# Residual rows of the first LayerNorm added to the expert sums inside rounds 0 and 1, and the routing lists made in one go

## The reference, cut to what matters

```python
x  = layer_norm(ALPHA * x + g1 * mix, ln1_g, ln1_b)          # x1, the residual rows spoken of below
u2 = x * (1 + sc2) + sh2
x  = layer_norm(ALPHA * x + g2 * hier_moe(u2, ...), ln2_g, ln2_b)

def hier_moe(u, ...):          # top-1 group of 4, then top-2 of its 8 experts; 32 experts in all
    g_idx = argmax(softmax(h @ w_gr + b_gr)); e_logits = h @ w_er + b_er
    top_val, top_idx = top_k(e_logits[group g_idx], 2)
    gate = g_w * softmax(top_val)
    for e in range(N_EXPERTS):
        hid = silu(h @ w_gate[e]) * (h @ w_up[e])            # 2048 -> 512
        y = y + dense_gate[:, e:e+1] * (hid @ w_down[e])     # 512 -> 2048
```

## Time and profile before

| | |
|---|---|
| time of the profiled execution, its span | 1728.13 us, 1726.0 us |
| median of three runs | 1728.73 us |
| TensorE matmul busy, share of span | 1568.4 us, 91% |
| VectorE busy | 532.8 us, 31% |
| ScalarE busy | 203.7 us, 12% |
| GpSimd busy | 88.4 us, 5% |
| moved by DMA, mean rate over the span | 537.01 MB, 311 GB/s |
| mean granted TensorE clock | 0.963 of 2.4 GHz |
| chain that ended last | PE 71%, DMA 17%, DVE 5% |

### The profile page before, as it was taken

How to read it: one execution, slowest core, us unless ns; L and a number is a source line. 1 busy time by engine, 2 the same in 40 slices (tenths; PEclk the granted TensorE clock), 3 DMA queues, 4 the chain that set the end, 5 groups by cost and what they waited for, 6 DMA issues and landing times.

```text
span 1726.0 us, 24825 instructions
## 1 busy us (share of the span) xinstructions
PE 1568.4 (91%) x9617; PEld 896.4 (52%) x9617; DVE 532.8 (31%) x948; ACT 203.7 (12%) x343; POOL 88.4 (5%) x174
## 2 busy tenths in 40 slices
PE   3799999999999998999977999999989889899893
PEld 0256666535777754577745444444435444344351
DVE  0110029611322324422164332323223232232325
ACT  0000010200000013320043000000000000100002
POOL 3000000000111100010001000000000000000000
PEclk8799999999999899899987999999999999999997
DMA  9999988875444363454336999999999999999991
GB/s 362 422 416 400 370 316 318 324 292 209 158 135 153 132 221 121 172 207 153 137 152 243 361 419 409 415 425 424 414 400 418 399 417 415 406 424 419 418 386 61
DMA packets 79394, 537.01 MB, mean 311 GB/s; under 512 B 10385, under 2 KB 10561, under 8 KB 18065
## 3 DMA queue, kind: packets, MB, share of 16 engines
q1 hardware_dynamic: 72146, 507.62, 73.5%
q0 software_dynamic: 6576, 26.35, 4.5%
q10 hardware_dynamic: 624, 2.36, 0.3%
HBM read 533.40 MB, written 11.80 MB: 316 GB/s over the span
## 4 chain that ended last, share of the span: by engine, by line
PE 71%; DMA 17%; DVE 5%; SPq 3%; ACT 2%; issue 2%; ACTq 0%; DVEq 0%
PE ps L616 15%; PE ps L1165 14%; DMA ring<-w_gate 12%; PE ps L1008 7%; PE ps L1190 6%; PE ps L629 6%; PE ps L600 4%; PE ps L1147 3%; SPq L407 3%; DMA ring<-w_ada 3%; DMA arena<-w_in 2%; PE ps L686 2%; PE ps L662 1%; PE ps L1117 1%; DVE arena L2037 1%
## 5 line engine op out<-in xcount | busy, mean ns | idle before, releaser
L1165 PE MATMUL ps<-ring,arena 128*64 128x256 f32 x3200 | 358.8, 383 | 21.2 <-DMA ring<-w_gate 20.0
L1165 PEld LDWEIGHTS ps<-ring,arena 128*64 128x64 f32 x3200 | 227.6, 138 | 167.8 <-DMA ring<-w_gate 33.3
L616 PE MATMUL ps<-arena,ring 128*128 128x288 f32 x1024 | 256.9, 409 | 0.0
L616 PEld LDWEIGHTS ps<-arena,ring 128*128 128x128 f32 x1024 | 191.9, 190 | 69.7 <-issue 18.4
L1190 PE MATMUL ps<-arena 128*64 128x512 f32 x800 | 181.5, 601 | 20.2 <-DVE arena L2055 12.9
L600 PE MATMUL ps<-ring,silu_c 128*32 128x512 f32 x768 | 103.7, 658 | 38.0 <-POOLq L513 19.4
L1008 PE MATMUL ps<-arena,ring 128*128 128x288 f32 x512 | 124.7, 406 | 0.0
L1190 PEld LDWEIGHTS ps<-arena 128*64 128x64 f32 x800 | 54.5, 138 | 131.2 <-issue 93.0
L629 PE MATMUL ps<-ring,arena 128*128 128x512 f32 x256 | 117.0, 605 | 1.3 <-ACT arena L1263 0.7
L1147 PE MATMUL ps<-arena 64*128 64x512 f32 x384 | 104.5, 636 | 12.3 <-DVE arena L2037 10.7
L1008 PEld LDWEIGHTS ps<-arena,ring 128*128 128x128 f32 x512 | 97.2, 190 | 26.8
(11 more groups left out here) (451 smaller groups left out, 1263.0 us busy)
## 6 DMA issues: line engine op xcount, KB each, us to landing
ring<-w_gate SPq DMA_DIRECT2D x100, 1024.0 KB, 23.5
ring<-w_up SPq DMA_DIRECT2D x100, 1024.0 KB, 25.8
arena<-w_down SPq DMA_DIRECT2D x100, 1024.0 KB, 26.4
ring<-w_ada SPq DMA_DIRECT2D x96, 1024.0 KB, 10.6
ring<-w_in SPq DMA_DIRECT2D x52, 1024.0 KB, 6.5
ring<-w_o SPq DMA_DIRECT2D x16, 1024.0 KB, 6.3
ring<-cache_k SPq DMA_DIRECT2D x16, 512.0 KB, 4.4
ring<-cache_v SPq DMA_DIRECT2D x16, 512.0 KB, 4.3
```

The source lines that it names most:

```text
L616: last = mm(ps[:, bank, 0:T], ring[:, slot, P * t:P * (t + 1)], uT[:, t, :], start=(t == 0), stop=(t == KC - 1))
L1165: last = mm(ps[B * s:B * (s + 1), 2 + c // 4, 0:256], xgT[:, 4 * (c % 4) + t, :], ring[:, c, 512 * t + 256 * s:512 * t + 256 * (s + 1)], s ...
```

## The change

1. VectorE makes the sample columns of each quarter of u2 right behind that quarter (`gain_sample(0)` first), not one quarter later.
2. TensorE makes the count product ahead of token turns 10 and 11, not behind turn 11.
3. The 12 turns of x1 leave the routing. The list product follows the token turns at once.
4. The expert of each block is counted on 41 partitions, one per block, and turned to a row by a small TensorE product with the identity; `plan` is written from that, now behind `idxs`.
5. GpSimd clears `acc[0]` and `acc[1]` (two more memsets behind that of `xg`). The turns of x1 stand at the end of round 0 (eight: rows 0 to 127 and the sample rows) and of round 1 (four: rows 128 to 255), in banks 4 and 7; VectorE adds them, times ALPHA, into `acc` or writes the sample rows, and TensorE waits for the last of them before it goes on to the next round.
6. `ln2b` is fetched by SyncE's queue behind the last expert, not by GpSimd's before the rounds. Buffers move in SBUF accordingly.

```diff
@@ buffers (some of them) @@
-        xgT = area(6656, KC, B)
+        xgT = area(18432, KC, B)
...
-        ln2b = area(18432, 2, D)
+        ln2b = area(4608, 2, D)
...
-        eid = rta(1624, NB1, parts=1)
-        ecmp = area(13824, NB1, NE, parts=1)
+        eid = rta(1624, 1)
+        ecmp = rta(1625, NE)
@@ SyncE, behind the loop over the experts @@
+            sp.wait_ge(tt_pe, 24)
+            sp.dma_start(ln2b, ln2.partition_broadcast(P)).then_inc(ln2_loaded, 16)
@@ GpSimd @@
             link(g.memset(xg, 0.0))
+            g.memset(acc[0], 0.0)
+            g.memset(acc[1], 0.0).then_inc(acc_clear, 1)
             pool.wait_ge(plan_ready, 1)
...
             gather(1)
-            pool.wait_ge(tt_pe, 24)
-            pool.dma_start(ln2b, ln2.partition_broadcast(P)).then_inc(late_loaded, 16)
@@ TensorE, routing @@
             for n in range(1, 12):
+                if n == 10:
+                    pe.wait_ge(rt_dve, 1)
...
                 turn_tokens(n, u2T)
...
-            for n in range(12, 24):
-                if n < 16:
-                    pe.wait_ge(x1_act, 4 * (n - 12) + 4)
-                if n == 16:
-                    pe.wait_ge(rt_dve, 2)
...
-                turn_tokens(n, rT)
+            pe.wait_ge(rt_dve, 2)
...
+            pe.wait_ge(rt_dve, 3)
+            mm(ps[0:1, 5, 0:NB1], eid[0:NB1, :], ident[0:NB1, 0:NB1], start=True, stop=True).then_inc(rt_pe, 1)
@@ TensorE, rounds @@
+            def turn_x1(first, i):
+                t0, tn = TILES[i]
+                for q in range(4):
+                    x = first + q
+                    if x >= 2:
+                        pe.wait_ge(xr_dve, x - 1)
+                    for m in range(4):
+                        last = nc.tensor.transpose(ps[0:tn, (4, 7)[x % 2], P * m:P * (m + 1)],
+                                                   rT[:, 4 * q + m, t0:t0 + tn], ident[:])
+                    last.then_inc(tt_pe, 1)
...
                         last.then_inc(moe_used, 1)
+                    with pe.If(i < 1):
+                        pe.wait_ge(x1_act, KC)
+                        turn_x1(0, 0)
+                        turn_x1(4, 2)
+                        pe.wait_ge(xr_dve, 8)
+                    with pe.If(i > 0):
+                        with pe.If(i < 2):
+                            turn_x1(8, 1)
+                            pe.wait_ge(xr_dve, 12)
@@ ScalarE @@
-            for n in range(12, 20):
...
-                A(xres[0:tn, i, :].rearrange("t (p m) -> t m p", m=KC)[:, 4 * q:4 * q + 4, :],
-                  ps[0:tn, 6 + n % 2, :].rearrange("t (m p) -> t m p", m=4), ACT.Copy, scale=ALPHA
-                  ).then_inc(tt_act, 1)
@@ VectorE @@
+            gain_sample(0)
             for q in range(1, 4):
                 centre(q)
                 scale_rows(q)
-                gain_sample(q - 1)
-            gain_sample(3)
+                gain_sample(q)
...
-            link(v.tensor_tensor(ecmp, bc(cum[0:1, :], 1, NB1), bc(iotab[0:1, 0:NB1], 2, NE), ALU.is_le))
+            link(v.tensor_scalar(ecmp, cum, tokid[:, 0:1], None, ALU.is_le))
             link(v.tensor_reduce(eid, ecmp, AX, ALU.add))
-            link(v.tensor_scalar(eid, eid, NE - 1.0, None, ALU.min))
-            v.tensor_copy(plan[0:1, 0:NB1], eid)
-            v.tensor_copy(plan[0:1, NB1:NB1 + 1], cum[0:1, NE - 1:NE]).then_inc(plan_ready, 1)
+            v.tensor_scalar(eid, eid, NE - 1.0, None, ALU.min).then_inc(rt_dve, 1)
             dve.wait_ge(rt_pe, 4)
...
+            dve.wait_ge(rt_pe, 5)
+            v.tensor_copy(plan[0:1, 0:NB1], ps[0:1, 5, 0:NB1])
+            v.tensor_copy(plan[0:1, NB1:NB1 + 1], cum[0:1, NE - 1:NE]).then_inc(plan_ready, 1)
...
+            def x1_rows(first, i):
+                for q in range(4):
+                    x = first + q
+                    dve.wait_ge(tt_pe, 13 + x)
+                    src = ps[0:TILES[i][1], (4, 7)[x % 2], :].rearrange("t (m p) -> t m p", m=4)
+                    if i == 2:
+                        v.tensor_scalar(xsrow.rearrange("t (p m) -> t m p", m=KC)[:, 4 * q:4 * q + 4, :], src,
+                                        ALPHA, None, ALU.mult).then_inc(xr_dve, 1)
+                    else:
+                        w = acc[i].rearrange("t (p m) -> t m p", m=KC)[:, 4 * q:4 * q + 4, :]
+                        v.scalar_tensor_tensor(w, src, ALPHA, w, ALU.mult, ALU.add).then_inc(xr_dve, 1)
...
                     v.tensor_tensor(yg[:, 512:1024], ps[:, 6, :], g2p[:, 512:1024], ALU.mult).then_inc(y_dve, 1)
+                    with dve.If(i < 1):
+                        x1_rows(0, 0)
+                        x1_rows(4, 2)
+                    with dve.If(i > 0):
+                        with dve.If(i < 2):
+                            x1_rows(8, 1)
```

More of the change, by code:

```diff
@@ L180, in layer @@
         xg = area(16384, D, parts=B)
-        xgT = area(6656, KC, B)
-        hid = area(7680, 256)
-        hsil = area(7936, 256)
-        hT = area(8192, 2, P)
+        xgT = area(18432, KC, B)
+        hid = area(19456, 256)
+        hsil = area(19712, 256)
+        hT = area(19968, 2, P)
         yout = area(13312, 1024)
@@ L191, in layer @@
         xsrow = xres[0:TS, 2, :]
-        ln2s = area(4608, 2, 512)
-        xs = area(5632, 512)
+        ln2s = area(20224, 2, 512)
+        xs = area(21248, 512)
         sum_s = area(28700, 512)
@@ L1084, in _ @@
             for n in range(1, 12):
-                turn_tokens(n, u2T)
[L1087 to L1093, removed]
-            last.then_inc(rt_pe, 1)
-            for n in range(12, 24):
-                if n < 16:
-                    pe.wait_ge(x1_act, 4 * (n - 12) + 4)
-                if n == 16:
-                    pe.wait_ge(rt_dve, 2)
[L1100 to L1104, removed]
-                turn_tokens(n, rT)
+                if n == 10:
+                    pe.wait_ge(rt_dve, 1)
+                    for i in range(3):
+                        mm(ps[:, 2, NE * i:NE * (i + 1)], causal[:, 0:P], both[:, i, :], start=True, stop=(i == 0))
+                        for k in range(i):
+                            mm(ps[:, 2, NE * i:NE * (i + 1)], ones[:], both[:, k, :], start=False, stop=(k == i - 1))
+                    for i in range(3):
+                        last = mm(ps[:, 3, 0:NE], ones[:], both[:, i, :], start=(i == 0), stop=(i == 2))
+                    last.then_inc(rt_pe, 1)
+                turn_tokens(n, u2T)
+            pe.wait_ge(rt_dve, 2)
+            for k in range(2):
+                for i in range(3):
+                    last = mm(ps[0:B, 4, 0:NB1], rsel[k][:, i, :], bsel[k][:, i, :],
+                              start=(k == 0 and i == 0), stop=(k == 1 and i == 2))
+            last.then_inc(rt_pe, 1)
+            pe.wait_ge(rt_dve, 3)
+            mm(ps[0:1, 5, 0:NB1], eid[0:NB1, :], ident[0:NB1, 0:NB1], start=True, stop=True).then_inc(rt_pe, 1)
             pe.sem_inc(moe_used, MOE_CHUNKS - SLOTS)
@@ L1172, in _ @@
                     with pe.If(i < 1):
-                        pe.wait_ge(tt_act, 20)
-                        pe.wait_ge(xr_dve, 4)
+                        pe.wait_ge(tt_act, 12)
+                        pe.wait_ge(idx_made, 1)
                         pe.wait_ge(diag_ready, 2)
@@ L1466, in _ @@
             nc.scalar.preload_act_table_set("natural_log_exp_and_others")
-            act.wait_ge(xr_dve, 4)
+            act.wait_ge(xr_dve, 12)
             for q in range(4):
@@ L2010, in _ @@
                     last.then_inc(diag_ready, 1)
[L2011 to L2016, removed]
             last.then_inc(diag_ready, 1)
@@ L2027, in _ @@
             nblocks = dve.value_load(plan[0:1, NB1:NB1 + 1], min_val=0, max_val=NBLK)
+            dve.wait_ge(acc_clear, 1)
+            def x1_rows(first, i):
[9 more added lines that the diff above has]
+                        v.scalar_tensor_tensor(w, src, ALPHA, w, ALU.mult, ALU.add).then_inc(xr_dve, 1)
             def add_piece(n, j):
```

8 lines of the change are left out of this document (3 added, 5 removed).

## The result

The changed kernel takes **1743.01 us** (median of five runs, 1739.05 to 1745.88) against 1728.73 (1723.39 to 1731.23) before: ratio 1.0087, 95% interval 1.0064 to 1.011. It is slower by 14.3 us; 7.6 were forecast, and the time lies above the range. The profiled execution took 1745.88 us, its span is 1744.1. A "stop" is the time for which TensorE's next round waits at the end of round 0 or 1, while the rows of x1 are turned and added.

The account below looks back on a forecast made before the run. The weight stream bounds the kernel from 1007 us; before that its empty queue near 973 us hangs on TensorE's round 1. Terms −5.5 + 8.9 + 3.2 + 1.0 = +7.6 on 1728.1 gave 1735.7 us, range 1729 to 1741.5.

Parts of the forecast that it names:

- round 0 earlier: Routing chain up to the turn of the first gathered rows: round 0 starts at 921.4 against 926.91, 5.5 us earlier.
- stop at the end of round 0: End of round 0: TensorE waits for eight x1 pieces on VectorE, 8.9 us late (8.5 to 10), nothing covering it.
- stop at the end of round 1, behind the cover: End of round 1: a 5.4 us wait, partly covered by the weight stream's lead, costs 3.2 us (2.5 to 4.5).
- Sample columns and count product (1, 2): Start of routing: logits 1.0 us earlier, count product gains 0.6 us more and ends at 903.3.
- Memsets beside the lists: Routing: three GpSimd memsets hold VectorE's first list mask until 911.2 instead of 908.2; lists ready at 913.3.
- x1 in rounds 0 and 1: Ends of rounds 0 and 1: TensorE waits for VectorE's x1 pieces, costing 8.9 and 3.2 us.
- Clock: First chunk's products and combine behind the x1 turns at half clock: between 0 and 3.5 us, 1.0 taken.
- Cover at round 1: Weight stream's lead at the end of round 1: 2.2 us, covering part of the 5.4 us stop.
- At nothing: Parts priced at zero: eight ScalarE copies dropped, three branches per round, `ln2b` fetched behind the last expert.
- weights ahead: Rival: chunks on their way cover TensorE's stops in early rounds, leaving only −5.5: 1722.6 us; chance 0.13.
- All bounds on the far side: Rival: pieces of 1.14 us, half clock at both ends, lists at 914: +13.2, 1741.3 us; chance 0.13.
- the last rival: Rival: first gather is no sooner, for instance because the last store lands late: −1 + 13.1, 1740 us; chance 0.06.

Follow-up runs that it names:

- late_plan_behind_gather: Changed kernel with x1 turns in rounds 11 and 17, `acc` memsets behind the first gather, GpSimd's `plan` reading there too, VectorE's ahead of copying `where`: 1722.02 us.
- keep_clock: Changed kernel plus extra unread 128x128 products between and behind the x1 turns, so TensorE stays busy in the stops: 1740.81 us, ratio 1.0074.
- x1_late: Changed kernel with the x1 turns and pieces moved from rounds 0 and 1 to the ends of rounds 11 and 17: 1726.07 us, ratio 0.9961.
- x1_rounds_2_3: Changed kernel with the x1 turns and pieces moved from rounds 0 and 1 to rounds 2 and 3: 1737.75 us, ratio 1.005.
- keep_clock_wait_at_combine: As keep_clock, with TensorE's wait for the last x1 pieces moved behind the next round's first chunk, ahead of combine: 1736.33 us, ratio 1.0047.
- no_x1: Changed kernel without x1 turns and their VectorE pieces (residual rows not added, sample rows zero): 1726.45 us, ratio 0.9976.
- late_plan_full_clock: late_plan_behind_gather plus 32 extra unread products ahead of the list product and 36 behind the expert-list turn: 1720.21 us, ratio 0.9949.

## Why the prediction was wrong in size

The direction and the mechanism held: an empty queue behind rounds 0 and 1, a stop of TensorE there that nothing covers, memsets that hold VectorE, and none of it if the stream is ahead. The sum was +7.6 and is +14.6 in the trace. Of the 7.0 us between them 1.8 are the routing's, 2.2 the first stop's, 1.3 those of round 0 and of the products behind that stop, and 1.7 the second stop's:

| term | forecast | measured, net | how |
|---|---|---|---|
| round 0 earlier | −5.5 | −3.7 | 924.93 − 1.75 against 926.91 |
| stop at the end of round 0 | +8.9 | +11.1 | first turn of x1 at 961.41 to the products at 972.48 |
| first chunk and combine at half clock, and a round 0 that is 0.4 longer | +1.0 for both ends | +2.3 | 9.7 + 3.7 − 11.1 |
| stop at the end of round 1, behind the cover | +3.2 | +4.9 | 14.6 − 9.7 |

- *Sample columns and count product (1, 2)*: right. The logits end net 0.9 us earlier (895.76 − 1.75 against 894.89), 1.0 was taken. The count product ends at 905.24, net 903.5; 903.3 was forecast.
- *Memsets beside the lists*: the hold was right, its size was not. The memsets began net 1.0 us later than worked out, mostly because the two token turns put behind the count product ran at half clock (1.89 us for both, against 1.22 in late_plan_behind_gather). The first mask then came net at 912.4 where 911.2 was taken, and the gather net at 919.0 instead of 917.7. The chain from list product to gather was right (4.2 us; 4.3 forecast); from the gather to the first turn it took 0.5 more (4.2 against 3.7), 0.3 of it in the landing. In the five other executions with this routing round 0 starts net 3.3 to 4.7 us earlier, so 5.5 was too much in each.
- *x1 in rounds 0 and 1, the step that failed.* The working followed VectorE and ended with its last piece plus 0.2 us. VectorE's part was right (0.96 us a piece with `acc`, 0.95 taken). Missing was TensorE's side: 1.56 us of loop instructions, which lay under running products before and lie bare behind a wait at the end of the loop's body, and half-clock turns that pace the last pieces (four in 4.32 us, up to 1.2 apart, instead of 3.52). These two, 1.4 and 0.8 us, are the 2.2 us by which the first stop is too long.
- *Clock*: named, but taken at 1.0 in all. At round 0 it alone is 1.8 us in the first chunk (3.68 against 1.89); at round 1 that chunk took 2.89 us. keep_clock removes both.
- *Cover at round 1*: 2.2 was taken, 3.3 was there; the stop, the first chunk and the combine were longer by more than that (8.2 against 5.4).
- *At nothing*: right; `ln2b`, 21.9 us from issue to landing behind the last expert, lands at 1711.4, ahead of its use at 1720.29 and later.
- *Rivals*: "weights ahead" would have needed a lead as long as the stop, which x1_late finds in round 11, not in rounds 0 and 1. "All bounds on the far side" is what came nearest (+13.2). Two of its terms came true, half clock (at the second end in part: 2.89 us) and late lists (ready at net 914.7); its slow pieces did not (0.96 us, not 1.14), and the loop instructions were in no term. The gather was in fact hardly sooner, as the last rival had it, but round 0 was, since the turns of x1 were out of TensorE's way.

## What to carry to other kernels

A stop of an engine is priced by the queue it stands in front of: the same two stops cost 17 us or more in two early rounds and nothing measurable once the weight queue held several chunks, so put such work where the queue is longest. Where a wait is put at the end of a loop's body, count the loop's own instructions and the clock of the first products behind it too; here a wait put behind the next independent products hid the loop's instructions, and products without use kept the clock. A memset on GpSimd is not free beside a chain of small VectorE instructions: three in a row cost 2.1 to 3.6 us more than one.

## What the runs showed of the hardware

A held VectorE instruction is not always let in between two memsets: L1993 began 0.74 us before the end of one memset and stayed until the end of the next, 2.51 us (L1994 behind it ends with it), while the instructions just before it, L1990 to L1992 (two inputs, or a reduction), ran beside a memset in 0.17 to 0.35 us each. The same 2.51 us stand in the traces of x1_rounds_2_3, keep_clock and keep_clock_wait_at_combine. In x1_late and no_x1 it is the first mask that is held through two memsets, for 3.32 us.

Which instruction is held hangs on hundredths of a microsecond. In the changed kernel L1988 starts 0.05 us ahead of the memset of `xg` and is held for 1.88 us, and the memset takes 1.80. In x1_late its like, L1989, starts 0.06 us ahead (908.30 against 908.36) and takes 0.16 us, and the memset 1.84.

The Trainium skill (SBUF — State Buffer, section "Who interferes with whom") has the hold as an exclusive lock that goes to whoever issues first. L1963 in the earlier trace rows, well inside its memset, agrees; for L1988 the recorded starts would have it the other way, and 0.05 us do not settle who issued first. L1993's record starts 0.68 us ahead of the memset that it waits for last, which looks as if the lock passed from GpSimd to GpSimd past a waiting VectorE; no run tests that reading.

TensorE at half clock in the routing carried it 7 us into round 0 (late_plan_behind_gather: granted 0.50 from 914 to 923 us, 0.54 from 923 to 930, 1.00 behind that); products without use in the idle time before kept it at 1.00 (late_plan_full_clock).
